# One decoder step on one core: the first compression round placed inside the input projection, the second amid long attention units, the output matrix loaded in halves

## The reference, cut to what matters

```python
n = rmsnorm(x)                                     # 576 rows
q, kv_cmp, kv_slc, kv_win, gates, u = split(n @ w_in)   # 1024 x 1816
# compression: every block of 64 positions to one key and one value
kc = einsum('bnlkd,lde->bnke', blk_k + pos, w_cmp_k)    # l = d = e = 64
vc = einsum('bnlkd,lde->bnke', blk_v + pos, w_cmp_v)
o_cmp, p = attention(q, rmsnorm(kc), vc)           # over blocks
idx = top_k(score(p), 16)                          # selected blocks
o = g0 * o_cmp + g1 * attention(q, selected blocks) + g2 * attention(q, window)
h = x + concat(o, pool_mix(u)) @ w_out             # 1024 x 1024
y = h + hier_moe(rmsnorm(h))                       # 16 experts, top 2 of one group of 4
```

## Time and profile before

| what | value |
|---|---|
| median of 3 runs | 784.98 us (784.39 to 786.95) |
| profiled execution | 788.33 us, span 786.7 us |
| TensorE busy | 730.6 us (93%) |
| VectorE busy | 267.7 us (34%) |
| GpSimd busy | 186.0 us (24%) |
| ScalarE busy | 172.1 us (22%) |
| mean granted TensorE clock | 0.965 |
| bytes moved | 191.76 MB, 244 GB/s over the span |

### The profile page before, as it was taken

The page is one execution under the profiler, slowest core; times in us unless marked ns, Lnnn a source line. Parts: engine busy times, 40 slices in busy tenths (PEclk is TensorE's granted clock), DMA queues, the critical chain, the costliest instruction groups (busy, mean ns, idle before and its releaser), DMA issues.

```text
span 786.7 us, 16071 instructions
## 1 busy us (share of the span) xinstructions
PE 730.6 (93%) x6460; PEld 411.3 (52%) x6460; DVE 267.7 (34%) x695; ACT 172.1 (22%) x367; POOL 186.0 (24%) x313
## 2 busy tenths in 40 slices
PE   6999998899889787888879999999999999999998
PEld 3555546656566554566735545345555544455542
DVE  1200071355647557766402337311111000111147
ACT  3100031344656533423201101101110011011000
POOL 2000044467667562644100000100000000000050
PEclk9999999989999659999989999999999999999999
DMA  9856645301910892656896019488999999999964
GB/s 282 228 163 210 202 105 116 121 2 56 318 58 17 260 338 65 174 155 186 231 408 271 27 55 357 166 319 318 402 407 419 428 414 424 420 420 419 393 251 144
DMA packets 74479, 191.76 MB, mean 244 GB/s; under 512 B 13718, under 2 KB 48806, under 8 KB 69917
## 3 DMA queue, kind: packets, MB, share of 16 engines
q1 hardware_dynamic: 62565, 154.82, 54.7%
q0 software_dynamic: 9600, 27.77, 10.4%
q10 hardware_dynamic: 2240, 8.13, 2.6%
HBM read 174.09 MB, written 16.70 MB: 243 GB/s over the span
## 4 chain that ended last, share of the span: by engine, by line
PE 77%; DVE 9%; issue 5%; DMA 5%; POOL 1%; ACT 1%; POOLq 1%; SPq 1%; DVEq 0%; ACTq 0%
PE bank L1319 30%; PE bank L879 13%; PE bank L1220 7%; PE bank L923 4%; PE bank L1027 2%; PE bank L876 2%; DMA arena<-in_w_out 2%; PE bank L1303 2%; DVE arena L1946 1%; PE bank L1166 1%; PE bank L1071 1%; PE bank L1040 1%; PE bank L1411 1%; PE bank L1211 1%; PE bank L1240 1%
## 5 line engine op out<-in xcount | busy, mean ns | idle before, releaser
L1319 PE MATMUL bank<-arena,proj 128*32 128x256 f32 (+1 forms) x2352 | 238.7, 483 | 1.3 <-DVE proj L2164 0.8
L1319 PEld LDWEIGHTS bank<-arena,proj 128*32 128x32 f32 x2352 | 103.6, 110 | 96.1 <-issue 77.7
L879 PE MATMUL bank<-arena,amT 128*128 128x454 f32 x256 | 101.1, 553 | 0.8 <-DVE amT L1661 0.8
L2352 POOL DMA_INDIRECT proj<-normed_rows,idx x12 | 11.4, 954 | 309.1 <-PE bank L1303 192.4
L2174 DVE TENSOR_TENSOR proj<-proj,bank 128x256 f32<-128x256 f32 x24 | 10.0, 422 | 209.8 <-PE bank L1319 209.8
L879 PEld LDWEIGHTS bank<-arena,amT 128*128 128x128 f32 x256 | 48.6, 193 | 49.2 <-issue 48.0
L1220 PE MATMUL bank<-arena,amT 128*128 128x512 f32 x128 | 57.8, 608 | 6.6 <-DMA arena<-in_w_out 6.6
L2291 POOL DMA_DIRECT2D arena<-in_cache_slc_kv x96 | 51.5, 536 | 52.5 <-issue 46.0
L1319 PE MATMUL bank<-amT,proj 128*32 128x512 f32 (+1 forms) x336 | 56.5, 532 | 0.0
L1319 PE MATMUL bank<-queries_and_bias,proj 128*32 128x512 f32 (+1 forms) x384 | 56.5, 486 | 0.0
L1220 PEld LDWEIGHTS bank<-arena,amT 128*128 128x128 f32 x128 | 24.5, 196 | 35.5 <-issue 28.7
(11 more groups left out here) (374 smaller groups left out, 1135.7 us busy)
## 6 DMA issues: line engine op xcount, KB each, us to landing
arena<-in_w_up SPq DMA_DIRECT2D x13, 2048.0 KB, 16.7
arena<-in_w_down SPq DMA_DIRECT2D x13, 2048.0 KB, 16.3
arena<-in_w_gate SPq DMA_DIRECT2D x10, 2048.0 KB, 17.1
arena<-in_cache_cmp_kv SPq DMA_DIRECT2D x96, 128.0 KB, 2.2
amT<-in_w_gate SPq DMA_DIRECT2D x3, 2048.0 KB, 14.5
queries_and_bias<-in_w_gate SPq DMA_DIRECT2D x3, 2048.0 KB, 11.7
expert_rows<-proj ACTq DMA_DIRECT2D x11, 512.0 KB, 9.7
arena<-in_w_in SPq DMA_DIRECT2D x3, 1816.0 KB, 7.5
```

The source lines that it names most:

```text
L879: last = pe.matmul(ps(("in", c, i))[0:n, 0:WC], xnT[:, k, i * P:i * P + n], w_in[c % 2][:, k, :], start=k == 0, stop=k == KC - 1)
L1319: ins = pe.matmul(dst[part, :], rows[:, part], own if q < TRIO else shared, start=start, stop=stop)
```

## The change

1. **Round 0 of the compression moves into the input projection.** `compress_within(c, i)` spreads its 64 steps over the last nine row-tile groups of the projection (from c = 2, i = 1), in two places of each group, at k = 2 and k = 6. Its weights come in four quarters of d through two buffers (`load_quarter`), and TensorE waits for each. SP issues requests 0 and 1 in one loop and quarter 0 ahead of `load_win(2)`; GpSimd issues requests 2 and 3 after `("in", 0, 1)`. GpSimd regroups round 0 before it norms the keys. Two chunk buffers move from `amT` to `queries_and_bias`.
2. **Banks.** The projection, mixer and q, k transposes rotate over six banks (`IN_BANKS`), since banks 4 and 5 hold the sums.
3. **Head norms.** The squares of q are taken one tile at a time through two small buffers.
4. **Round 1** moves from units 15 to 19 to units 5 to 9, and the block chain from units 21 to 32 to units 11 to 20. Requests 4 and 5 are issued separately (`load_later`), request 5 behind the pool stores; the whole `w_cmp` matrices come behind it.
5. **The output matrix** is loaded in two parts: rows 512 to 1023 (2 MB, three transfers) in the sample attention at t = 2, the other eight transfers where they were. It lies in three places (`out_matrix`). `norm2_g` shares the semaphore of the second load of x. Expert slots 1 and 0 swap their turns, and load n = 4 no longer waits for the output projection.

The diff, cut to its core:

```diff
-CMP_UNITS = [(0, 6), (15, 5)]
+CMP_UNITS = [(0, 0), (5, 5)]
-BEFORE = 3
+EARLY_GROUPS = 9
+QUARTER = 16
+IN_BANKS = (0, 1, 2, 3, 6, 7)
...
-def compress_before(i):
+def compress_within(c, i):
-    return [(0, d) for d in range(BEFORE * i, BEFORE * (i + 1))]
+    k = (c - 2) * TILES + i - (2 * TILES - EARLY_GROUPS)
+    return share([(0, d) for d in range(HD)], EARLY_GROUPS, k) if k >= 0 else []
...
-    21, 22, 25, 26, 28, 29, 23, 29
+    11, 12, 14, 15, 16, 17, 13, 17
...
-            load_cache(0, 0, 2)
+            for par in range(2):
+                sp.dma_start(posr[64 * par:64 * par + 64, :], a["cmp_pos_emb"]).then_inc(ld_pos, 16)
+            load_cache(0, 2)
+            sp.wait_ge(act_sq, TILES)
+            filled(sp, ("xT", TILES - 1, 1))
+            load_quarter(0)
             filled(sp, ("in", 0, TILES - 1))
             load_win(2)
-            load_cache(0, 2, 2)
+            load_quarter(1)
             filled(sp, ("in", 1, TILES - 1))
             load_win(3)
-            sp.wait_ge(heads_ms, 1)
-            load_wcmp(1)
...
+            for q in (2, 3):
+                sp.wait_ge(chunk_used, QUARTER * (q - 1))
+                load_quarter(q)
+            sp.wait_ge(regrouped, regrouped_at(0, HD - 1))
+            load_later(4)
             filled(sp, ("in", 3, TILES - 1))
             sp.dma_start(sel[0:NS, :, :], a["c_sel"]).then_inc(ld_sel, 16)
-
-            load_wcmp(0)
...
+            load_later(5)
+            for par in range(2):
+                filled(sp, ("cmp", 0, par))
+            load_wcmp(1)
+            load_wcmp(0)
...
                 filled(sp, ("slc_k", t - 2, 3, 1))
                 load_slc(2 * t, 0, 1)
+                if t == 2:
+                    for k in range(KVH):
+                        filled(sp, ("p_T", NP - 1, k))
+                    filled(sp, ("p_o", NW - 1))
+                    sp.wait_ge(st_out, 16 * N_OUT)
+                    sp.dma_start(w_out_late, a["w_out"][512:768, :].rearrange("(k p) c -> p k c", p=P)).then_inc(ld_wout, 16)
+                    for k in range(2):
+                        src = a["w_out"][768 + P * k:768 + P * (k + 1), :].rearrange("p (h c) -> p h c", h=2)
+                        sp.dma_start(w_out_rows[:, 2 * k:2 * k + 2, :], src).then_inc(ld_wout, 16)
...
-            sp.dma_start(w_out[:, 4:8, :], a["w_out"][512:1024, :].rearrange("(k p) c -> p k c", p=P)).then_inc(ld_wout, 16)
...
                     for k in range(KC):
+                        if c >= 2 and k % 4 == 2:
+                            for r, d in share(compress_within(c, i), 2, k // 4):
+                                compress(r, d)
...
+                if r == 0 and d % QUARTER == 0:
+                    pe.wait_ge(ld_quarter[d // QUARTER % 2], 64 * (d // QUARTER // 2 + 1))
...
-                for r, d in compress_before(i):
-                    compress(r, d)
...
+            raw(0)
             for i in range(TILES):
                 n = ROWS[i]
                 filled(ve, ("kT", i))
...
+            filled(po, ("in", 0, 1))
+            cmp_pages(2)
+            cmp_pages(3)
...
+            for d in range(HD):
+                regroup(0, d)
+
             po.wait_ge(heads_rt, 2)
...
+            po.wait_ge(regrouped, regrouped_at(0, HD - 1))
+            cmp_pages(6)
+            cmp_pages(7)
```

214 lines of the change are left out of this document (112 added, 102 removed).

## The result

The changed kernel takes 799.23 us (median of 4, 795.19 to 799.94) beside 785.97 us for the kernel before on the same chip: ratio 1.0157, 95% interval 1.0114 to 1.02. It is slower, by about 13 us, where 15 us less were forecast; the time lies outside the range of 758 to 783. The profiled execution took 799.26 us with a span of 797.6.

A forecast was written before the change was run, and what follows sets the result against it. TensorE, busy 730.6 of 786.7 us, was taken as the bound, with idle time and low clock to win. 17.5 + 1.7 - 3.6 - 7.6 + 2.9 - 22 + 3 - 6.6 = -14.7 gave 770.3 us, range 758 to 783.

The forecast's parts named there:

- Round 1's data: Second compression round: pages ready to copy at 185, weights landed at 188, TensorE there at 196; no wait, margin 8 us.
- Round 1 comes late: Rival: second compression round's weights land near 215, TensorE stands in unit 5 for 20 us; total 792 us; chance 0.08.
- The third quarter of w_in: Input projection: this load lands near 72.3 us, with a megabyte in front of it; +1.7 us, between 0 and 4.
- Round 0 in the projection: Input projection: 64 compression steps in 18 places add 17.5 us, between 16 and 20.
- The rival that let each switch expose a whole product: Input projection: 36 switches to and from compression steps cost 0.38 us each, 13.7 us more; total 784 us; chance 0.06.
- Units 0 to 5: Prompt attention, now without compression steps: 17.5 us instead of 25.1, so -7.6 us, between -6.6 and -10.
- Units 5 to 10: Prompt attention with the second round's compression steps: 31.8 us.
- tail: Prompt attention from unit 20, without block chain: 25.5 us for 47.5, -22, between -17 and -24; 3 us given back for clock.
- The chain: Block chain in units 10 to 20 of the prompt attention: 35 us, between 31 (all covered) and 48 (nothing covered).
- the chain keeps its price: Rival: block chain in units 10 to 20 not covered, clock falls as before, 48 us not 35; total 780; chance 0.14.
- The output matrix: Wait of 6.63 us for w_out goes: -6.6 us, between -5.8 and -6.6; some 1.7 us more possible, not counted.
- the rival with the chain covered whole: Long units fill every gap around the block chain, clock stays high, 31 us not 35; total 760; chance 0.20.

The follow-up runs named there:

- the two pairs of runs: Block chain put back to units 21 and on: with the selection matrix ahead of the weights, ratio 1.0003 beside 0.9953; on the changed kernel, 1.0235 beside 1.0157.

## Why the prediction was wrong

Its own milestones against the trace. The prediction's are the numbers of its steps, put end to end:

| stretch | predicted, us | measured, us | difference |
|---|---|---|---|
| start to first scores | 168.2 | 177.04 | +8.8 |
| first scores to Round 1 reached | 27.8 | 23.5 | -4.3 |
| wait at Round 1 | 0 | 18.2 | +18.2 |
| units 5 to 10 with Round 1 | 31.8 | 32.6 | +0.8 |
| units 10 to 20 with the chain | 35 | 45.5 | +10.5 |
| units 20 to the sample attention (with the 3 us for clock) | 28.5 | 24.1 | -4.4 |
| from there to the first expert product | 193.2 | 191.0 | -2.2 |
| first expert product | 484.5 | 512.0 | +27.4 |

**The step that failed is "Round 1's data"**: "Both come before 196, so no wait; the margin is 8 us." It added issue times to a landing of 9.9 us, which the earlier trace rows show for weights on queues with little else to do, and 4.37 us for pages. In the changed kernel the weights took 15.6 and 24.9 us and GpSimd's last pages 16.1 in the median, 24.2 for the last. GpSimd's copy was to run at 185 and ran at 216.4: 11 of these 31 us are late issue (its last page by 192.1, where the step has about 181), 20 are the landing, and TensorE, which was there at 200.6, stood for 18.2. The step counted when transfers are issued, where it had to count what is still to be moved. The rival that did count them, "Round 1 comes late", got 792, its mechanism (4 transfers in one queue behind the pages, 20 us of wait) and its 15 us of wait at which the change starts to lose nearly right, and a chance of 0.08. Its other figure, 45 us for 10.5 MB, 197, is when the data is there once the engines are kept busy from Round 0's end on: 196 to 199 in six of the runs. That it fits is luck: SyncE issues 32 pages after Round 0 and not 16 (12.6 MB with the weights, besides the stores), and over 148 to 200 us the run with the selection matrix ahead moved 274 GB/s, not 233. The margin was not 8 us, it was none, even with the best order: with the distances early TensorE stood at Round 1 from 195.3 to 198.8.

**The third quarter of w_in**: right in kind (a megabyte in front of it), wrong in size. It was taken as +1.7, at most 4; it was 5.35 of idle time and about 3 us of clock behind it (half clock from 75.0 to 81.9). It took 14.74 us to land, and in the run that put it in front 10.12, with 2 MB behind it, where it took 7.5 before: so by my estimate 4.6 us are the megabyte in front and 2.7 what shares the engines. That run gave both back, 7.5 us at the first scores; the 8.1 at the first expert product agree with it, as far as that place can tell.

**Round 0 in the projection**, +17.5: right for the places themselves, too low for the whole. Places of 3 steps took 0.82 us and of 4 steps 1.05, from the chain of the changed kernel, with no wait for chunks or weights quarters anywhere:

```profile
86.75 0.82 PE bank L910 x24
87.58 3.25 PE bank L941 x8
90.83 1.05 PE bank L910 x32
```

Eight of the first and ten of the second are 17.1. But the eight products between two places take 3.25 us, where eight of the 64 before took 3.08: the switch also costs something outside the place. In the run with the third quarter in front, which has neither wait nor low clock here, the time from the third quarter's first product to the mixer's is 77.5 us where it was 57.1 before: 20.4, just outside the 16 to 20. The rival that let each switch expose a whole product, 13.7 us, falls all the same: it is about 3.

**Units 0 to 5** were better than said, 3.2 us each and not 3.5, and 3 us more went ahead of unit 0's transposes, which came 7.5 us behind the first scores and not 10.5. **Units 5 to 10** and the **tail**, without the 3 us given back for clock, were right within 1 and 2 us.

**The chain**: the forecast had half of the units' extra work fall into idle time and the clock mostly up, 35 us. It took 45.5, near the end "nothing covered and the same clock" (48). This term too was mis-sized, and at its clock: 0.81 over this stretch means, with the two levels, some 17 us of it at the lower one, which by my estimate is worth up to 9 us; two waits of 2.15 us remain. That the chain is better off among long units is shown by the two pairs of runs, worth 5 to 6 us. The rival "the chain keeps its price" had the size nearly right, at 0.14, though not its condition, the clock as before (0.66).

**The output matrix**, -6.6: right, and more than the 1.7 us "I do not count" were there too: 10 us in the stretch by the run that took it back. The loads that moved forward disturbed nothing that TensorE shows: its longest waits in the sample attention are 1.55 us, as before.

One sum of the prediction is off besides: the rival with the chain covered whole adds up to 23.7 us and 761, not 25 and 760. It changes nothing.

So of the 27 us, 18 are the wait at Round 1 and 10 the chain; w_in's 7 and Round 0's 3 nearly cancel with the gains in the units and behind them. With the order mended, the first expert product comes at 493.9, 5.5 us before the old 499.39 and 9 behind the forecast, and what is left of the change is small.

## What to carry to other kernels

Before work is moved ahead of its data, count the bytes that may start only after the same event, divide them by the rate that the windows show for transfers of the same kind (here 208 to 226 GB/s beside the weights and 359 to 388 without them, the engines full in both), and compare that with the arrival of the engine; the time to landing of a single transfer is that of its company, and it does not move with the transfer. When loads are put in a new order, list every small load behind them in the issuing engine's program: a selection matrix of 128 KB cost as much (16.4 us) behind a full queue as the megabytes had. A queue of its own did not help the small load here; an earlier moment took its wait away.
